# Token-major projections in units of 512 columns and half the rows, in place of 256 columns and all rows

## The reference

```python
# first block (once)
h = rms_norm(x, norm1_g); z = h @ w_in                      # 1024 -> 2560
a, gate, q, k, v = split(z)                                 # 512 columns each
conv_out = silu(layer_norm(depthwise_conv31(a * sigmoid(gate))))
q, k = rms_norm per head; attn_out = neighbourhood_attention(q, k, v, rpb)
x = x + concat(conv_out, attn_out) @ w_out
h = rms_norm(x, norm2_g); x = x + (silu(h @ w_gate) * (h @ w_up)) @ w_down     # 2816
# second block (two layers)
u = rmsnorm(x, norm_mix); proj = u @ w_in_2                 # 1024 -> 5444
q, k, v, iq, ik, iw, cB, cC, ch, g = split(proj)            # 512 512 512 256 64 4 512 512 512 2048
q, k, iq, ik = apply_partial_rope(...)
score = sum_h relu(iq_h . ik) * iw_h   # 4 index heads; the 64 best keys of each token are kept
y_attn = attention(q, k, v | kept keys) @ w_attn_out
y_conv = (cB * short_conv(cC * ch)) @ w_conv_out
x = x + (sigmoid(g0) * y_attn + sigmoid(g1) * y_conv) @ w_mix_out
x = x + square(relu(rmsnorm(x) @ w_up)) @ w_down            # 4096
# at the end
return rmsnorm(x, norm_final)
```

## Time and profile before

| | |
|---|---|
| three runs | 1071.69, 1072.92, 1077.14 us |
| profiled execution | 1077.12 us |
| its span, first to last instruction | 1075.3 us |
| PE busy | 1044.9 us, 97% |
| DVE, ACT, POOL busy | 708.1, 538.7, 69.6 us |
| DMA | 185.21 MB, mean 172 GB/s |
| chain that ended last | PE 87% of the span |

### The profile page before, as it was taken

How to read it: one execution, slowest core, us unless ns; L and a number is a source line. 1 busy time by engine, 2 the same in 40 slices (tenths; PEclk the granted TensorE clock), 3 DMA queues, 4 the chain that set the end, 5 groups by cost and what they waited for, 6 DMA issues and landing times.

```text
span 1075.3 us, 17550 instructions
## 1 busy us (share of the span) xinstructions
PE 1044.9 (97%) x6689; PEld 921.8 (86%) x6689; DVE 708.1 (66%) x1073; ACT 538.7 (50%) x707; POOL 69.6 (6%) x80
## 2 busy tenths in 40 slices
PE   8989989999998999999999999999999999999997
PEld 6975778888888999998788888799999987888886
DVE  5886767666667576768666656466877676665654
ACT  6555565444446544455634444375354546444433
POOL 0000000000000308000000000002080000000000
PEclk9999999999999999999999999999999999999999
DMA  9974335555475564149465563765532674656520
GB/s 284 204 241 161 118 119 196 196 191 194 132 219 169 160 179 137 61 166 299 140 205 187 186 205 93 232 189 162 161 116 79 209 262 151 201 179 212 159 95 39
DMA packets 141922, 185.21 MB, mean 172 GB/s; under 512 B 6409, under 2 KB 126879, under 8 KB 141855
## 3 DMA queue, kind: packets, MB, share of 16 engines
q1 hardware_dynamic: 141767, 184.25, 54.4%
q10 hardware_dynamic: 88, 0.04, 0.0%
HBM read 180.91 MB, written 1.56 MB: 170 GB/s over the span
## 4 chain that ended last, share of the span: by engine, by line
PE 87%; DVE 3%; ACT 3%; SPq 2%; DMA 2%; issue 2%; ACTq 0%; DVEq 0%
PE wide L541 17%; PE wide L513 10%; PE wide L515 9%; PE wide L514 9%; PE acc L513 9%; PE acc L514 9%; PE acc L515 9%; PE wide L542 8%; ACT whi L982 2%; DVE wlo L1289 1%; DMA raw<-in_w_in 1%; SPq L434 1%; PE acc L674 1%; PE acc L708 1%; PE acc L695 1%
## 5 line engine op out<-in xcount | busy, mean ns | idle before, releaser
L1289 DVE TENSOR_TENSOR wlo<-raw,whi 128x2048 fp32r<-128x2048 f32 (+1 forms) x178 | 386.8, 2180 | 164.2 <-ACT whi L982 163.2
L982 ACT ACTIVATE whi<-raw 128x2048 fp32r<-128x2048 f32 (+1 forms) x178 | 322.3, 1818 | 97.5 <-PE wide L515 44.7
L541 PE MATMUL wide<-uhl,whi 128*128 128x512 f32 x864 | 307.7, 399 | 4.4 <-DVE wlo L1289 4.4
L542 PE MATMUL wide<-uhl,wlo 128*128 128x256 f32 x864 | 242.4, 281 | 0.0
L541 PEld LDWEIGHTS wide<-uhl,whi 128*128 128x128 f32 x864 | 162.4, 188 | 44.9 <-DVE wlo L1289 5.7
L542 PEld LDWEIGHTS wide<-uhl,wlo 128*128 128x128 f32 x864 | 163.3, 189 | 1.4
L513 PE MATMUL wide<-uhl,whi 128*128 128x256 f32 (+1 forms) x528 | 152.5, 289 | 0.8 <-DVE wlo L1374 0.8
L514 PE MATMUL wide<-uhl,whi 128*128 128x256 f32 (+1 forms) x528 | 150.3, 285 | 0.0
L515 PE MATMUL wide<-uhl,wlo 128*128 128x256 f32 (+1 forms) x528 | 150.2, 285 | 0.0
L513 PE MATMUL acc<-whi,mhi 128*128 128x512 f32 x376 | 147.8, 393 | 1.8 <-DVE wlo L1289 1.6
L514 PE MATMUL acc<-wlo,mhi 128*128 128x512 f32 x376 | 146.8, 390 | 0.0
(11 more groups left out here) (251 smaller groups left out, 1288.1 us busy)
## 6 DMA issues: line engine op xcount, KB each, us to landing
raw<-in_w_in SPq DMA_DIRECT2D x51, 1024.0 KB, 5.4
raw<-in_w_mlp_up SPq DMA_DIRECT2D x32, 1024.0 KB, 6.0
raw<-in_w_mlp_down SPq DMA_DIRECT2D x32, 1024.0 KB, 4.9
raw<-in_w_gate SPq DMA_DIRECT2D x11, 1024.0 KB, 5.4
raw<-in_w_up SPq DMA_DIRECT2D x11, 1024.0 KB, 5.4
raw<-in_w_down SPq DMA_DIRECT2D x11, 1024.0 KB, 5.5
raw<-in_w_mix_out SPq DMA_DIRECT2D x8, 1024.0 KB, 6.0
raw<-in_w_out SPq DMA_DIRECT2D x4, 1024.0 KB, 8.2
```

The source lines that it names most:

```text
L541: pe.matmul(col[2 * n + c][:], whi_v(u)[:, f, cs], uhl[:, f, :], start=start, stop=False)
L542: return pe.matmul(col[2 * n + c][:, 0:T], wlo_v(u)[:, f, cs], uhl[:, f, 0:T], start=False, stop=stop)
L982: act.activation(whi[:, u.buf, 0:size], raw[:, u.slot, 0:size], ACT.Copy).then_inc(w_hi, 1)
L1289: dve.tensor_tensor(wlo[:, u.buf, 0:size], raw[:, u.slot, 0:size], whi[:, u.buf, 0:size].bitcast(F32), ALU.subtract).then_inc(w_lo, 1)
```

## The change

Units 4 to 9 of the first block and 2 to 7 of each layer hold all 512 columns of q, k or v and 4 of the 8 row blocks: unit 4 is q on row blocks 0 to 3, unit 5 q on row blocks 4 to 7, and so on. The bytes per unit are the same; the rows of a load are 2 KB each where they were 1 KB. Token half t accumulates in a whole bank over two units, so that two banks belong to one tensor. A unit is 24 matmuls of 512 columns: first 16 with the high weights (uhi, then ulo), which wait for `w_hi` alone, then 8 with the low weights, which wait for `w_lo`. ACT empties two banks with two instructions of 512 columns, after the second unit of each pair.

Units 0 and 1 of a layer hold the 324 columns of iq, ik and iw together, on row blocks 0 to 3 and 4 to 7. Index keys come out token-major, so that their copy, their transposes and two semaphores go. The matmuls of these units wait chunk by chunk for the row block and token half that they read.

```diff
-L_COLS = [IK0, IQ0, 0, 256, 512, 768, 1024, 1280, CC0, CC0 + 256, CH0, CH0 + 256, CB0, CB0 + 256] \
-    + [G0 + COLS * i for i in range(8)]
-A_COLS = [512, 0, 768, 256, 1024, 1280, 1536, 1792, 2048, 2304]
+IDXW = CB0 - IQ0
+L_TOKEN_COLS = [IQ0, 0, DA, 2 * DA]
+A_COLS = [512, 0, 768, 256]
+A_TOKEN_COLS = [1024, 1536, 2048]
...
-            if layer and j == 0:
-                return KD * IKW
+            if layer and j < 2:
+                return KD // 2 * IDXW
...
+                    h, at = j % 2, A_TOKEN_COLS[j // 2 - 2]
+                    load(a_unit(j), w_in[:, 4 * h:4 * h + 4, at:at + DA])
...
-            def col_tokens(u, bank, between=None):
-
+            def token_half(u, h, banks, n=DA, k=None, between=None):
+
+                wh, wl = (w[:, u.buf, 0:KD // 2 * n].rearrange("p (k n) -> p k n", n=n) for w in (whi, wlo))
+                pe.wait_ge(w_hi, u.upto())
                 for t in range(NT):
-                    tok = slice(t * P, t * P + P)
-                    for k in range(KD):
-                        mm = mm3(bank[:, t * COLS:t * COLS + COLS], uhi[:, k, tok], ulo[:, k, tok],
-                                 whi_v(u)[:, k, :], wlo_v(u)[:, k, :], k == 0, k == KD - 1)
+                    for f in range(4):
+                        tok = slice(t * P, t * P + P)
+                        if k is not None:
+                            pe.wait_ge(u_lo, chunk_count(k, 2 * h + t, f))
+                        pe.matmul(banks[t][:, 0:n], uhi[:, 4 * h + f, tok], wh[:, f, :], start=h == 0 and f == 0, stop=False)
+                        pe.matmul(banks[t][:, 0:n], ulo[:, 4 * h + f, tok], wh[:, f, :], start=False, stop=False)
                     if t == 0 and between:
                         between()
+                pe.wait_ge(w_lo, u.upto())
+                for t in range(NT):
+                    for f in range(4):
+                        mm = pe.matmul(banks[t][:, 0:n], uhi[:, 4 * h + f, t * P:t * P + P], wl[:, f, :],
+                                       start=False, stop=h == 1 and f == 3)
                 mm.then_inc(used, 1)
...
-                if 4 <= j < 8:
-                    pe.wait_ge(fevac, j - 3)
-                if j >= 8:
-                    pe.wait_ge(evac, j - 7)
+                if j in (4, 6):
+                    pe.wait_ge(fevac, j - 2)
+                if j == 8:
+                    pe.wait_ge(evac, 1)
...
+                pe.wait_ge(evac, A_TOKENS - 1 if p == 0 else A_TOKENS)
                 if p == 0:
-                    pe.wait_ge(evac, A_TOKENS)
...
-                        col_tokens(u, col[j % 4])
+                    if j < 2:
+                        token_half(u, j, col[0:2], IDXW, k, None if j else lambda: turn_quarter(k, 3))
+                    elif j < L_FIRST:
+                        n = j // 2 % 2
+                        token_half(u, j % 2, col[2 * n:2 * n + 2])
...
-                    if j == 1:
-                        pe.wait_ge(ik_sb, l + 1)
-                        for t in range(NT):
-                            tr = pe.transpose(acc[1][:, t * IKW:t * IKW + IKW], ikf[0:IKW, t * P:t * P + P],
-                                              ident[0:IKW, 0:IKW])
-                        tr.then_inc(ik_ps, 1)
...
+            def evacuate_tokens(u, j, dst):
+
+                act.wait_ge(used, u.upto())
                 for t in range(NT):
-                    out = act.activation(dst[:, t, :], col[j % 4][:, t * COLS:t * COLS + COLS], ACT.Copy, scale=rn[:, t:t + 1])
+                    out = act.activation(dst[:, t, :], col[j // 2 % 2 * 2 + t][:], ACT.Copy, scale=rn[:, t:t + 1])
                 out.then_inc(evac, 1)
...
-                elif j >= 4:
-                    if j == 4:
+                elif j in (5, 7, 9):
+                    if j == 5:
                         act.wait_ge(diag_ok, 1)
-                    evacuate_scaled(u, j, half((qtok, ktok, vtok)[(j - 4) // 2], j % 2))
+                    evacuate_tokens(u, j, (qtok, ktok, vtok)[j // 2 - 2])
...
-                    if j == 0:
+                    if j == 1:
                         act.wait_ge(used, u.upto())
-                        act.activation(ikf[0:IKW, :], col[0][0:IKW, 0:T], ACT.Copy).then_inc(ik_sb, 1)
-                    elif j == 1:
-                        evacuate_scaled(u, j, iqtok)
-                        act.wait_ge(ik_ps, l + 1)
                         for t in range(NT):
-                            act.activation(iktok[:, t, 0:64], ikw[:, t, 0:64], ACT.Copy, scale=rn[:, t:t + 1])
-                            out = act.activation(iw[:, t, :], ikw[:, t, 64:68], ACT.Copy, scale=rni[:, t:t + 1])
+                            act.activation(iqtok[:, t, :], col[t][:, 0:256], ACT.Copy, scale=rn[:, t:t + 1])
+                            act.activation(iktok[:, t, 0:64], col[t][:, 256:320], ACT.Copy, scale=rn[:, t:t + 1])
+                            out = act.activation(iw[:, t, :], col[t][:, 320:IDXW], ACT.Copy, scale=rni[:, t:t + 1])
                         out.then_inc(evac, 1)
```

More of the change, by code:

```diff
@@ L64 @@
 LOOPS = 5
-IQ0, IK0, CB0, CC0, CH0, G0 = 1536, 1792, 1860, 2372, 2884, 3396
-IKW = 68
-L_COLS = [IK0, IQ0, 0, 256, 512, 768, 1024, 1280, CC0, CC0 + 256, CH0, CH0 + 256, CB0, CB0 + 256] \
-    + [G0 + COLS * i for i in range(8)]
-A_COLS = [512, 0, 768, 256, 1024, 1280, 1536, 1792, 2048, 2304]
+IQ0, CB0, CC0, CH0, G0 = 1536, 1860, 2372, 2884, 3396
+IDXW = CB0 - IQ0
+L_TOKEN_COLS = [IQ0, 0, DA, 2 * DA]
+L_COLS = [CC0, CC0 + 256, CH0, CH0 + 256, CB0, CB0 + 256] + [G0 + COLS * i for i in range(8)]
+A_COLS = [512, 0, 768, 256]
+A_TOKEN_COLS = [1024, 1536, 2048]
 A_OUT_ROWS = [2, 3, 0, 1]
@@ L79 @@
 L_FIRST = 8
[L80 removed]
+A_TOKENS, A_FEATURES = 3, 4
+L_TOKENS = L_FIRST // 2
 L_FEAT = L_CONV - L_FIRST
@@ L442, in _ @@
             for j in range(1, A_OUT):
-                load(a_unit(j), w_in[:, :, A_COLS[j]:A_COLS[j] + COLS])
+                if j < len(A_COLS):
+                    load(a_unit(j), w_in[:, :, A_COLS[j]:A_COLS[j] + COLS])
+                else:
+                    h, at = j % 2, A_TOKEN_COLS[j // 2 - 2]
+                    load(a_unit(j), w_in[:, 4 * h:4 * h + 4, at:at + DA])
                 if j == 1:
@@ L484, in _ @@
                 for j in range(L_CONV):
[L485 to L488 removed]
+                    h, at = j % 2, (L_TOKEN_COLS[j // 2] if j < L_FIRST else L_COLS[j - L_FIRST])
+                    if j < L_FIRST:
+                        n = IDXW if j < 2 else DA
+                        load(l_unit(l, j), of(w_in2)[:, 4 * h:4 * h + 4, at:at + n], KD // 2 * n,
+                             None if j == 2 else l_unit(l, 2 if j == 1 else j))
+                    else:
+                        load(l_unit(l, j), of(w_in2)[:, :, at:at + COLS])
                 for at, w in ((L_CONV, w_conv2), (L_ATTN, w_attn2)):
@@ L755, in _ @@
                 else:
-                    col_tokens(u, col[j % 4], between=first_scores if j == A_OUT - 1 else None)
+                    n = j // 2 % 2
+                    token_half(u, j % 2, col[2 * n:2 * n + 2], between=first_scores if j == A_OUT - 1 else None)
                 if j == 0:
@@ L839, in _ @@
             last_rows([(a_unit(A_UNITS - 1), mid(mhi, 0), mid(mlo, 0))])
-            def first_units(l):
+            with pe.Fori(0, LAYERS) as l:
                 k = 2 + 2 * l
-                u, v = l_unit(l, 0), l_unit(l, 1)
-                hi, lo = ikw_v(whi[:, u.buf, :]), ikw_v(wlo[:, u.buf, :])
                 for i in range(3):
                     turn_quarter(k, i)
-                pe.wait_ge(w_lo, u.upto())
-                for h in range(2):
-                    for f in range(4 * h, 4 * h + 4):
-                        pe.wait_ge(u_lo, feature_count(k, f))
-                        mm = mm3(col[0][0:IKW, 0:T], hi[:, f, :], lo[:, f, :], uhi[:, f, :], ulo[:, f, :],
-                                 f == 0, f == KD - 1)
-                    if h == 0:
-                        turn_quarter(k, 3)
-                        pe.wait_ge(w_lo, v.upto())
-                    else:
-                        mm.then_inc(used, 1)
-                    for t in range(NT):
-                        tok = slice(t * P, t * P + P)
-                        for f in range(4 * h, 4 * h + 4):
-                            mm = mm3(col[1][:, t * COLS:t * COLS + COLS], uhi[:, f, tok], ulo[:, f, tok],
-                                     whi_v(v)[:, f, :], wlo_v(v)[:, f, :], f == 0 and t == 0, f == KD - 1 and t == 1)
-                mm.then_inc(used, 1)
@@ L867, in _ @@
-            with pe.Fori(0, LAYERS) as l:
-                first_units(l)
-                for j in range(1, L_CONV):
+                for j in range(L_CONV):
                     u = l_unit(l, j)
-                    if j > 1:
+                    if j >= L_FIRST:
                         pe.wait_ge(w_lo, u.upto())
-                    if 4 <= j < 12:
-                        pe.wait_ge(evac, A_TOKENS + L_FIRST * l + j - 3)
+                    if j in (4, 6, 8, 10):
```

(5 more changed lines are left out.)

42 lines of the change are left out of this document (11 added, 31 removed).

## The result

| | runs | median, us | lowest to highest |
|---|---|---|---|
| before | 11 | 1075.27 | 1071.69 to 1078.06 |
| after | 11 | 1067.93 | 1064.78 to 1069.87 |

The ratio is 0.9924, with a 95% interval of 0.9911 to 0.9937: the kernel is 8.2 us faster, where 14.6 were forecast. The time forecast was 1058.3 us, in a range up to 1065.5; 1067.93 lies above it. 2.4 of the 9.6 us between the two are the start of the sum: three runs of before had their median at 1072.92, eleven at 1075.27. The rest is the change itself, which gave little more than half.

A forecast was written before the change was run, and what follows sets the result against it. PE's instruction stream, busy 97% of the span, was taken to bound the kernel. Layers 11.0 plus first block 3.6 gave 14.6 us off the 1072.92 us median: 1058.3 us, range 1054.5 to 1065.5.

The forecast's parts named there:

- The layers: Both layers: head 3.3 us plus six units at 0.36 us gain 5.5 us each, 11.0 us in all.
- The pitch of 324 columns: Units 0 and 1 of a layer: matmuls start 0.149 us apart, on a line between 0.121 and 0.227.
- The head: Units 0 and 1 of a layer: 48 matmuls and no PE wait left, 3.3 us earlier.
- the unit: Units 4 to 9 and 2 to 7: 5.45 us of PE time for 5.81, 0.36 us less each.
- Up to `convolve(0)`: First block: copies of cu issued 5 us earlier let the convolution start 2.5 us earlier; 0.4 us more from the clock.
- Rival A: First block: copies land no earlier, `convolve(0)` at 57.8 us again, clock falls as before; gain 11.7 less up to 0.5; 27%.
- The clock: Convolution behind PE's wait: half clock cost 1.1 us; 0.4 of 0 to 1.1 us taken as gain.
- Units 7 to 9: First block, up to the second pair's scores: 0.7 us gained, with PE waiting some 0.7 us for kT.

The follow-up runs named there:

- heads_alone: The changed kernel with 7 matmuls of zeros on PE in the 1.88 us wait at the head of each layer: 1068.24 us, ratio to before 0.9927.
- block_only: The kernel before with the change in units 4 to 9 of the first block alone, layers as before: 1078.63 us, ratio to before 1.0014.
- warm: The changed kernel with 16 matmuls of zeros on PE between unit 6 and `convolve(0)`: 1066.22 us, ratio to before 0.9907.
- layers_only: The kernel before with the change in the two layers alone, first block's units 4 to 9 as before: 1065.62 us, ratio to before 0.9910.
- conv_late: The changed kernel with `convolve(0)` and `convolve(1)` moved from after unit 6 to after unit 7: 1062.65 us, ratio to before 0.9879.
- loads_after_copies: The changed kernel, where SP waits until all 16 copies of cu have landed before issuing load 9 and those of w_out: 1064.26 us, ratio to before 0.9890.

## Why the forecast was wrong

**The layers** were right in mechanism, and a little too large: 5.0 us each for 5.5. No wait took the gain, the low weights and the chunks came in time. The pitch of 324 columns was 0.148 to 0.15 (forecast 0.149). The head gained 3.1 us for 3.3. The term mis-sized is the unit: 0.30 us, not 0.36. The two durations that I subtracted were not alike. The 0.121 us of before were taken over 96 matmuls from the first of unit 5 on, whose start behind other work they hold; the 0.227 were taken inside a long row of equals. Over the same two units, 353.92 to 364.94, the new matmuls are 11.02 / 48 = 0.230 us apart. From unit 0 to q's transposes it is 38.34 us, 37.9 forecast.

**Up to `convolve(0)`** is the step that failed: 2.5 us for the copies and 0.4 for the clock. I took it that copies issued 5 us earlier land 2.5 us earlier. Over all the profiles they were issued about 5 us earlier (7.6 in the first pair) and landed no earlier. I didn't ask what SP issues behind them. Load 9 and two of w_out moved up by 7 us with them: before, 10 of the 16 copies had landed when SP issued load 9 at 53.1 us, in the changed kernel 2 at 46.2, and the last copy's 5.29 us became 10.94. Rival A said that the copies would not land earlier; it priced this at 11.7 us by letting units 7 to 9 keep their 0.7, and at a clock that falls "as before". The runs went past A: the first block alone is at -1.5 us, between +0.1 and -3.1 by its interval, under the -0.5 that I had called its floor.

**The clock** was taken as a term between 0 and 1.1 us. It costs 1.3 us in the convolution of the kernel before (4.92 us from 57.87 to unit 7 where 3.59 is full speed), 1.7 in the changed kernel's profile, and 2.1 in that of heads_alone. What I missed is that it differs from execution to execution behind the same wait, and that the kernels with the longer wait ran at the lower mean clock (0.992 in block_only, 0.995 in before beside it). The eleven executions of the changed kernel go with it: the three shortest, 1064.78 to 1065.87 us, had mean clocks of 0.998, 0.997 and 0.994, the four at 0.992 took 1068.90 to 1069.87. It is not the whole of it: 1066.83 and 1069.58 both had 0.993. The profiled one was among the short ones, and the profiled one of before among the long ones of its kernel. That their clock makes all of this difference isn't shown; the zeros at the heads alone didn't help, those ahead of the convolution did, as far as two intervals that just overlap can say.

The Trainium skill (TensorE: Matmul & The Clock Gate, section What's actually happening) says that the same kernel can run a different number of matmuls at the lower clock from one execution to the next, according to the phase of the hardware's monitor when the kernel starts. The trace agrees for the start: the changed kernel and warm, which are the same up to 51 us, had their clock rise at 9.3 and at 15.8 us. What the runs show beyond it is the same in the middle of the kernel: behind the same 1.88 us of idle at layer 0's head, layers_only ran at 0.50 and the changed kernel at 1.00.

**Units 7 to 9.** PE waits 0.61 us for kT ahead of the first scores, 0.7 forecast. From the end of the convolution to the second pair's scores it is 21.0 us; before it was 84.24 - 62.79 = 21.5 (62.79 is where unit 7 starts in the trace of before). 0.4 to 0.5 gained, 0.7 forecast.

**The sum.** 14.6 forecast, less 1.0 for the layers and 5.1 for the first block, gives 8.5; measured 8.2. The -1.5 of the first block and the 8.2 are each known to about 1.5 us, so that they meet this closely is partly luck.

**The range** was too narrow on one side. A's chance of 27% belonged to something worse than A, and I had no case for a first block that loses. The chance of faster was 0.91; it came out 0.8% faster, not far beyond the 0.5%.

## To carry to other kernels

- When a change lets a queue run ahead, list everything that the queue issues next, behind the transfer you care about too. Early loads that nobody waits for can hold back the small transfer that somebody does; a wait on the queue until it has landed gave 3 to 4 us here.
- Time saved ahead of a wait is lost if what is waited for comes no earlier, and with a clock that falls behind idle PE it can be worse than lost (block_only, 1.5 us slower). Put the waiting work behind the next piece that doesn't need it (conv_late, 5 to 7.5 us), or fill the wait.
- Before a gain under 1% is read from one profile each, look where each profiled execution lies among its kernel's runs: the two here differ by 11.6 us, the medians by 7.3.

## What I had not expected of the hardware

**The end of the copies is one engine's work.** In loads_after_copies nothing else is moved from 51.8 us on, while the last copies land. The DMA view from 50.5 to 54.5 us (busy tenths and GB/s in 40 slices):

```profile
DMA  3423231100100000000000000000000000000000
GB/s 89 132 100 111 100 109 66 55 21 20 41 20 23 23 23 23 23 23 23 23 23 23 23 23 23 23 23 23 34 23 23 23 23 23 23 23 23 23 23 23
```

For over 3 us 23 GB/s are moved, at a busy share of 0.06 to 0.07, one sixteenth: 1136-byte packets of 51 ns, each beginning as the one before ends. All 16 copies had been issued by 48.2 us; the last landed at 55.3. By the share and the packets' order, a single engine of the 16 was behind; the trace doesn't name the engine of a packet. Which packets had put it behind was not tried.

**Packets are slowed by their company.** A 2048-byte packet took 84 to 88 ns (median) where loads had the engines to themselves, and 245 ns from 51 to 54 us in the changed kernel, among 1136-byte packets of the copies that took 144 ns where they take 51 alone. In that stretch DMA was fully busy by its share and moved 140 GB/s, against 355 to 407 with 2 KB loads alone, from 37 to 42 us.
